# Mixed K and V inputs made earlier, accumulation banks taken by age, and small weights and side work moved, in a two-block fp32 kernel

## What is computed

```python
h = _rms(x, norm_mix_pre[layer]) * (1 + sc_m) + sh_m
xx = _token_shift(h) - h
x_rkv = h[None] + xx[None] * mu[:3, None, None, :]
r, k, v = jnp.einsum("nbtd,nde->nbte", x_rkv, w_rkv)      # three products, 2048 x 2048 each
w = -jax.nn.softplus(-(w0 + jnp.tanh(xw @ w1) @ w2)) - 0.5
a = jax.nn.sigmoid(a0 + (xa @ a1) @ a2)
...
y = _rwkv7_scan(rh, heads(decay), kh, vh, -kk, kk * ah)
...
x = x + g_m * _rms(y @ w_o, norm_mix_post[layer])
u = _causal_dwconv(h @ w_in, conv_w, conv_b)              # FFN's first product, 2048 x 11008
gate, val = jnp.split(u, 2, axis=-1)
f = (jax.nn.silu(gate) * val) @ w_out                     # FFN's second product, 5504 x 2048
```

## Time and profile before

| | us |
|---|---|
| median of three runs | 3032.55 |
| the three runs | 3032.55, 3021.90, 3033.14 |
| the profiled execution | 3020.16 |
| its span on the core | 3018.2 |
| TensorE busy in the span | 2813.4 (93%) |
| VectorE busy | 1869.0 (62%) |
| ScalarE busy | 1283.6 (43%) |
| GpSimd busy | 100.8 (3%) |
| mean granted TensorE clock, of full | 0.958 |
| DMA over the span | 514.11 MB, mean 170 GB/s |

### The profile page before, as it was taken

One profiled execution on the slowest core, in us unless ns is written; L12 is line 12 of the kernel. 1 busy time (PEld: TensorE's weight loads), 2 busy tenths in 40 slices (PEclk: granted clock), 3 DMA queues, 4 the chain that ended last, 5 costly groups with the idle time before them and its releaser, 6 DMA issues.

```text
span 3018.2 us, 45825 instructions
## 1 busy us (share of the span) xinstructions
PE 2813.4 (93%) x19618; PEld 2380.1 (79%) x19618; DVE 1869.0 (62%) x2460; ACT 1283.6 (43%) x1735; POOL 100.8 (3%) x127
## 2 busy tenths in 40 slices
PE   6999986898988899999989999999999999999997
PEld 2487875777877688788878878888978888888886
DVE  3776745676655577657757656566657556566554
ACT  1243423333214655445425545456555444343443
POOL 0101101111000000000000000000000000000000
PEclk9999997898889999999999999999999999999999
DMA  9766642232216266666665554443444555555552
GB/s 380 252 237 205 209 167 67 85 111 78 79 64 212 95 226 193 223 212 207 224 194 182 183 180 131 165 145 106 132 146 165 192 186 187 173 191 182 169 194 84
DMA packets 289212, 514.11 MB, mean 170 GB/s; under 512 B 10097, under 2 KB 122737, under 8 KB 288881
## 3 DMA queue, kind: packets, MB, share of 16 engines
q1 hardware_dynamic: 286016, 500.21, 49.4%
q0 software_dynamic: 2560, 7.90, 0.8%
q10 hardware_dynamic: 432, 3.07, 0.3%
HBM read 508.91 MB, written 2.10 MB: 169 GB/s over the span
## 4 chain that ended last, share of the span: by engine, by line
PE 81%; DVE 8%; ACT 5%; issue 3%; DMA 2%; POOL 0%; DVEq 0%; SPq 0%; ACTq 0%
PE ps L767 43%; PE ps L769 21%; PE ps L733 2%; PE ps L906 1%; DMA RAWa<-in_ada_w 1%; PE ps L901 1%; DVE WLb L1702 1%; ACT WHb L1195 1%; PE ps L676 1%; PE ps L891 1%; PE ps L794 1%; PE ps L868 1%; PE ps L858 1%; PE ps L788 1%; PE ps L957 1%
## 5 line engine op out<-in xcount | busy, mean ns | idle before, releaser
L767 PE MATMUL ps<-XB,WHb 128*128 128x512 f32 x2304 | 831.6, 404 | 30.1 <-DVE WLb L1702 19.2
L769 PE MATMUL ps<-XB,WLb 128*128 128x256 f32 x2304 | 646.8, 281 | 0.0
L1702 DVE TENSOR_TENSOR WLb<-RAWb,WHb 128x2048 fp32r<-128x2048 f32 (+1 forms) x196 | 426.2, 2191 | 315.5 <-ACT WHb L1195 315.3
L767 PEld LDWEIGHTS ps<-XB,WHb 128*128 128x128 f32 x2304 | 437.4, 190 | 138.2 <-issue 24.5
L1702 DVE TENSOR_TENSOR WLd<-RAWd,WHd 128x2048 fp32r<-128x2048 f32 x144 | 328.6, 2290 | 325.6 <-ACT WHd L1195 325.6
L1195 ACT ACTIVATE WHb<-RAWb 128x2048 fp32r<-128x2048 f32 (+1 forms) x196 | 356.8, 1832 | 332.4 <-PE ps L769 330.5
L767 PE MATMUL ps<-XD,WHd 128*128 128x512 f32 x1280 | 461.9, 403 | 4.1 <-DVE R L1754 3.2
L769 PEld LDWEIGHTS ps<-XB,WLb 128*128 128x128 f32 x2304 | 439.3, 191 | 1.2
L1195 ACT ACTIVATE WHd<-RAWd 128x2048 fp32r<-128x2048 f32 x144 | 274.8, 1915 | 364.9 <-PE ps L769 364.9
L767 PE MATMUL ps<-FB,WHd 128*128 128x512 f32 x1024 | 364.8, 400 | 2.7 <-DVE UM L2309 2.7
L769 PE MATMUL ps<-XD,WLd 128*128 128x256 f32 x1280 | 361.0, 282 | 0.0
(11 more groups left out here) (329 smaller groups left out, 3518.6 us busy)
## 6 DMA issues: line engine op xcount, KB each, us to landing
RAWb<-in_ffn_w_in SPq DMA_DIRECT2D x168, 512.0 KB, 5.1
RAWd<-in_w_up SPq DMA_DIRECT2D x64, 1024.0 KB, 5.2
RAWd<-in_w_down SPq DMA_DIRECT2D x64, 1024.0 KB, 5.1
RAWa<-in_ada_w SPq DMA_DIRECT2D x48, 1024.0 KB, 7.4
RAWa<-in_rwkv_w_rkv SPq DMA_DIRECT2D x48, 1024.0 KB, 5.8
RAWb<-in_ffn_w_out SPq DMA_DIRECT2D x36, 1024.0 KB, 5.2
RAWs<-in_ada_w SPq DMA_DIRECT2D x32, 1024.0 KB, 5.1
RAWb<-in_w_in SPq DMA_DIRECT2D x44, 512.0 KB, 4.8
```

What stands on the lines that cost most here:

```text
L767: pe.matmul(bank[:, :], WH[tag][:, w, o:o + P], acts(k), start=(k == 0), stop=False)
L769: mm = pe.matmul(bank[:, 0:T], WL[tag][:, w, o:o + P], acts(k)[:, 0:T], start=False, stop=last)
L1702: dve.tensor_tensor(WL[tag][:, n % WN, 0:size], RAW[tag][:, slot, 0:size], WH[tag][:, n % WN, 0:size].bitcast(F32), ALU.subtract).then_inc ...
```

## The change

1. `xa_mix` writes the K inputs into the K array and the V inputs into HV, in place, not into MX, two tiles per chunk in the second and third group of the product before. The hook of the fourth group keeps the copies to XA and their rests. K holds the low-rank weights LG1 until the 48th low-rank step, for which VectorE waits once. The MX ring numbers of later stages shift by 32.
2. Banks are handed out by age: a tile takes the bank that was given out longest ago (of those that its product may use). The list starts anew at R, W_o, the first FFN product, `g_p` and `g_o2`.
3. In block one's FFN the 16 modulation items stand behind the third and fourth chunk of each group of the first two second products.
4. TensorE sums a finished piece when it comes to the item's own place (`walk_to(place[...])`), not two chunks ahead; VectorE reads the columns when it is three items past the piece.
5. `accumulate` is split: a group's first tile is added up before VectorE's next split, the other three behind it.
6. W2 and A2 get memory outside the buffers of the R, K and V products. GpSimd loads them before the barrier, and M64 before it, too, behind the last V mix.

```diff
-        for n, c in enumerate([c for f1, f2 in g_f for c in flat(f1) + flat(f2)]):
-            stream += [c] + ([rest.pop(0)] if rest and n % 6 == 5 else [])
+        for f1, f2 in g_f:
+            stream += flat(f1)
+            for chunks in f2.groups:
+                for ci, c in enumerate(chunks):
+                    stream += [c] + ([rest.pop(0)] if rest and ci > 1 else [])
...
+        by_age = []
         for gm in [g_r, g_k, g_v, g_o] + [x for p in g_f for x in p] + [g_p, g_o2] + [x for p in g_m for x in p]:
+            if gm in (g_r, g_o, g_f[0][0], g_p, g_o2):
+                by_age = list(range(7))
             for i in range(gm.tile0, gm.tile_end):
-                b = (i - gm.tile0) % {g_p: 6, g_r: 5}.get(gm, 7)
+                b = next(b for b in by_age if b < {g_p: 6, g_r: 5}.get(gm, 7))
+                by_age.remove(b)
+                by_age.append(b)
                 tile_bank.append(b)
...
+        def mix_of(which, j):
+            if which == "r":
+                return MX[:, mx_no("r", j) % 4, :]
+            return K[:, j, :] if which == "k" else HV[:, j, 1:T + 1]
...
                     for ci, ch in enumerate(chunks):
-                        walk(min(ch["number"] + 2, limit - 1))
+                        walk_to(place[ch["number"]])
                         tag = tag_of(place[ch["number"]])
...
+            walk_to(end_r)
             barrier(pe, tally)
...
-            def ada_finish():
-                while unread:
-                    piece = unread.pop(0)
+            def ada_finish(now=None):
+                while unread and (now is None or unread[0][1] + 3 <= now):
+                    piece = unread.pop(0)[0]
...
-                    if i % 2 and i >= EARLY + 2:
-                        ada_finish()
+                    if i >= EARLY + 2:
+                        ada_finish(i)
...
                     for ci, ch in enumerate(chunks):
                         last = ch is chunks[-1]
+                        if last and evac is accumulate:
+                            accumulate(gm, g, 0, 1)
                         if last and g in evac_first:
                             evac(gm, g)
                         walk(min(ch["number"] + 2, limit - 1))
                         if hook:
                             hook(g, ci)
-                        if last and g not in evac_first:
+                        if last and evac is accumulate:
+                            accumulate(gm, g, 1, n_tiles(gm, g))
+                        elif last and g not in evac_first:
                             evac(gm, g)
...
             def xa_mix(which, j):
                 dve.wait_ge(s_sh, shift_at[which] + j + 1)
-                u = mx_no(which, j)
-                if u >= 4:
-                    dve.wait_ge(*mx_done[u - 4])
-                mixed(MX[:, u % 4, :], j, cols_of[which], xx_at[which] + j)
+                if which == "r" and mx_no("r", j) >= 4:
+                    dve.wait_ge(*mx_done[mx_no("r", j) - 4])
+                mixed(mix_of(which, j), j, cols_of[which], xx_at[which] + j)
...
             def mix_hook(which):
                 def hook(g, ci):
-                    for j in range(4 * ci, 4 * ci + 5) if g == 3 else []:
-                        if j < 4 * ci + 4:
+                    if g in (1, 2):
+                        if which == "k" and g == 1 and ci == 0:
+                            dve.wait_ge(s_lora, 3 * ND)
+                        for j in range(2 * (4 * g - 4 + ci), 2 * (4 * g - 4 + ci) + 2):
                             xa_mix(which, j)
-                        if j > 4 * ci:
-                            xa_lo(which, j - 1)
+                    if g == 3:
+                        for j in range(4 * ci, 4 * ci + 4):
+                            xa_lo(which, j)
...
             for stage in ("r", "k", "v"):
                 for j in range(ND):
                     shifted(stage, j)
+            load_wa(0)
+            pool.wait_ge(s_mix, mix_no("v", ND - 1))
+            pool.dma_start(M64, A["m64"][:, 0:T]).then_inc(s_m64, 16)
             barrier(pool, tally)
-            pool.dma_start(M64, A["m64"][:, 0:T]).then_inc(s_m64, 16)
-            load_wa(0)
             load_g(0)
```

19 lines of the change are left out of this document (9 added, 10 removed).

## The result

The changed kernel takes 2950.24 us in the median of four runs (2946.05 to 2959.37); the four runs of the kernel before, among them one more than the table above has, have their median at 3027.23. The ratio is 0.9752, with a 95% interval of 0.9714 to 0.979: 77 us less by the medians, where the prediction had 62 less from the profile and 2964 as its time. The profiled execution is the longest of the four, 2959.37 with a span of 2957.5; the prediction's sum against the profile was 2958.

The account below looks back on a forecast made before the run. The prediction held that time can fall only where TensorE waits. Its terms summed to 65.0 us, less 3 in charges: 62 us, giving 2958 from the profile or 2970 from the median; it took the middle, 2964, range 2944 to 2988.

Parts of the forecast that it names:

- Rival C: Second products: transfers of modulation items make TensorE wait, slower than before; 3041 us if transfers take 18 us; chance 0.04.
- (1): K and V products: inputs mixed earlier and banks by age remove the waits at their start; 16.0 us with clock.
- the crowded groups: Groups two and three, which take the moved mixes: second tiles may get banks late; 1 us charged for each.
- rival A: Groups two and three: VectorE and GpSimd exclude each other at SBUF; some 8 us less gain, 2972 us; chance 0.09.
- Both causes go: Before K and V: ScalarE's late evacuation and the bank still in use both end; 11.3 us of waits.
- (2): Modulation columns at their own place: four accumulator waits and the low clock behind two go; 11.8 us.
- (3): Scan's start: first weights loaded before the barrier, so ScalarE's sigmoid starts 8.3 to 8.6 us earlier; 8.5 taken.
- (4): FFN boundaries: banks by age and one tile added before the split remove evacuation waits; 26.7 us with clock.
- (5): Modulation items moved into second products: a 4.5 us wait for a split falls to 2 to 2.5; 2.0 us gained.
- The third charge: Many small boundaries: 1 us taken off the sum for what is late next there.
- two places: Three runs of the kernel before, read as lying at 3021.9 and 3033; the forecast took the middle of 2958 and 2970.
- Rival B: ScalarE's evacuation stays late, so waits return at the fourth tile; 21 us of gain lost, 2985 us; chance 0.09.

Follow-up runs that it names:

- b_banks: The kernel before with only banks handed out by age, mixes still in the fourth group and all additions behind the split: median 3002.11 us, ratio 0.9908.
- a_banks_old: The changed kernel with the banks of before (tile number modulo 7, from 0 in each product): median 2979.23 us, ratio 0.9823 to the kernel before.
- a_items_dense: The changed kernel with all 16 modulation items in the first second product, one behind every chunk: median 2964.24 us, ratio 0.9798 to the kernel before.

## Why the prediction came out as it did

The sign, the mechanisms and the range were right; the time came out 14 us lower than the forecast by the first median, 12 by the median of eight runs. One sign of a rival appeared, on a small scale (C, below). Point by point:

(1) Right. No wait before K and V, full clock. The stretch gained 284.2 - 248.7 = 35.5 us in all, of which 9.8 are the columns and 8.3 the weights, so 17.4 are its own, where the sum had 16.0 and took 2 off for the crowded groups (the two profiles of the kernel before are 1.8 us apart in this stretch, so the 17.4 is no sharper than that). The charge was not needed: no wait of 0.2 us or more in these groups, so rival A decided nothing, though the port's price can be seen. Which half did it, I had left open ("Both causes go"); the runs say the mixes, 11.8, and the banks 2.2 to 3.6, which leaves 2 us or more that neither run accounts for; the early mixes without any other part were not run. In the expectation of b_banks I had it wrong.

(2) Right in size between R and scan (10.0 against 9.8) and right that the clock follows from the wait. In FFN 1 it was 5.2 against 1.8, 1.2 of it a wait that part 4 counts.

(3) The mechanism right, the term 1.2 too small: 9.7. The prediction priced the low clock behind the other waits and left it out behind this one, the longest, where the granted clock was 0.50.

(4) All nine waits are gone, and the order of the first addition was needed (11.5 us in block one). That rested on an argument which held only together with the banks; the prediction's price of the split ("needed at 5.5") looked at TensorE's need of the split, not at the additions behind it, which a_banks_old shows to be the real cost.

(5) 1.9 us against 2.0; the wait 2.65 where I wrote 2 to 2.5. The new wait of 0.42 and 1.33 us is this part's price, and is in the 1.9.

**What was mis-sized is the price of a wait.** The sum took each at the length that the profile prints. The row behind says more. Before, around the first of the four waits for UM (timeline of TensorE):

```profile
2350.27 0.28 PE L769 MATMUL ps<-XD,WLd 128*128 128x256 f32 x1
2351.22 0.47 PE L767 MATMUL ps<-FB,WHd 128*128 128x512 f32 x1 [0.67 <-DVE UM L2309]
2351.53 0.28 PE L769 MATMUL ps<-FB,WLd 128*128 128x256 f32 x1
```

In an unbroken stream the second would start 0.12 us behind the first and the third 0.24 behind the second; here it is 0.95 and 0.31. So 0.90 us are lost to a wait printed as 0.67, because the printed wait begins at the modelled end of a matmul that in a stream overlaps the next. The same sum gives 0.22 to 0.27 us over the printed wait at the other waits of up to 2.1 us for an evacuation, in both profiles of before, and 0.49 or 0.50 at the three longest, where the matmul behind it already runs at the low clock. It was not worked out for the waits for accumulators and A2, whose instructions are others. 0.23 us each, as an estimate for all 23 waits that went (9 + 3 + 1 for the evacuations of block one's and two's products into R and K, 4 for UM, 1 for UT, 4 for accumulators, 1 for A2), is 5.3 us. FFN 2 shows it by itself: seven waits of 6.5 us in all and one low clock of 1.7 make 8.2, with 7 x 0.23 = 1.6 it is 9.8, and 10.8 were gained.

The account of the profiles, corrected for the pace: 35.5 (R to scan) + 1.4 (the scan's first round) + 24.9 (FFN 1) + 10.8 (FFN 2) = 72.6 us, against 62. The difference of 10.6 is 5.3 for the restarts, 2 for the charges in the two crowded groups that nothing came of, 1.2 for part 3, and about 2 that stay unexplained. The third charge, 1 us for what is late next at the small boundaries, was met by the new wait of 0.42 and 1.33 us. With 73 in place of 62 the same median of the three runs gives 2960, and the median of 27 runs, 3029.45, gives 2956; 2952.3 was measured. The last 4 us are less than what the scan's clock (11 us) and the pace (up to 8 us) do between two executions of one kernel. The choice of the middle between profile and median rested on "two places" that do not exist; it took off 6 us for a reason that was none, and by luck in the right direction.

That the sum against the profile, 2958, met the first profiled execution of the changed kernel, 2959.37, is luck too. The two first profiles are 60.7 us apart. Of the 72.6 gained, 8.2 are hidden because the kernel before ran 504 pairs at the long pace in the two stretches and the changed kernel 1740, and 2.6 because the changed kernel's scan was the longer one (468.3 against 465.8).

Rival B did not come: no wait moved to a fourth tile, since the late evacuation that it feared hangs on the ring, which was gone; b_banks is the kernel in which it is real. Rival C did not come in its size, but its sign did: the prediction named as such a sign that ScalarE's copies in the second products wait for a DMA. They do, 28.6 us in the changed kernel and none in the kernel before, and what TensorE lost by it is 0.42 to 1.33 us. The transfers there took 6.1 and 6.6 us where the prediction had taken 5.2 from the kernel before. a_items_dense shows that twice as many items per group cost 12 us, at landings of 6.6 us, far below the 16.2 that the rival asked for.

## What to carry to other kernels

A wait of an engine that streams costs its printed length, the overlap that is lost at the restart (0.23 us here), and often some microseconds of low clock: price it by start-to-start distances, not by the printed wait. Where one wait has two causes in a row (a bank chosen badly, an evacuation that is late), mend the late engine first: here the late evacuation was worth 11.8 us and the bank 2.2. An operation put ahead of another for the sake of one reader delays all that stand behind: here, in block two, it costs nothing with an allocation by age, and loses 6.3 us without it. Work that is moved to where an engine has time brings its transfers along: look at the copies' waits for DMA there, not only at the engine's own time.

## What the hardware showed that was not expected

TensorE's stream of fp32r pairs has two paces at the same granted clock of 1.00: 0.3467 and 0.3533 us for a pair of 512 and 256 columns (1.9% apart). One of the two sets in behind an interruption and stays until the next; which one differs between executions, but in block two's last 750 us it was the long one in all fourteen profiles. By the table's counts, 11.5 and 12.6 us of the changed kernel's two profiles went to the longer pace between R and the scan and in FFN 1; in the first profile of before it was 3.3, in the second 11.7. What decides it is open; no experiment was made on it. The Trainium skill ("TensorE: Matmul & The Clock Gate", section "Back-to-back issue gap") gives a formula for the gap of a matmul by itself, with one value for each number of columns; the estimate by it for such a pair is 325 ns, below both paces, and no run here shows that figure.

And the clock does not fall behind every wait: of two equal waits of 1.59 us in the kernel before, the granted clock in the six microseconds behind reads 0.72 and 1.00.

```profile
2811.70:2817.70 6.00, 5.86 (x32) 4.89 (x32) 2.84 (x3) 0.45 (x1) 0.00 (x0) 1.00 0.60 199
```
